# Another order of the same operations in the middle stage of a two-layer hybrid decoder step

## The chip, the cores and the metric

The kernel runs on one core of one Trainium2 chip. The metric is device time in microseconds (us). Before the change it is 1229.5 us, the median of three runs (1227.54 to 1229.52). Engines are named as in the profile: PE is TensorE's matmul, PEld its weight load, DVE is VectorE, ACT is ScalarE, POOL is GpSimd, SP is SyncE, which here issues every DMA; a small q behind a name (SPq) means the sequencer of that engine.

## The reference, cut to what matters

There are two layers. Each layer takes 512 prompt tokens (four tiles of 128 rows) and 64 sample tokens (8 sequences of 8 new tokens, the fifth tile, `S_TILE`) and does this:

```python
h = rmsnorm(x);  z = h @ w_in                      # one product makes all branch columns
q_r, k_r, v_r, g_r, q_lat, c_raw, kpe_raw, g_a = split(z)
# retention: 4 heads, chunks of 128 tokens, one state of 128 x 128 per head
a = (q_r k_r^T) * decay mask;  o = a v_r + q_r S * decay;  S = S * decay + k_r^T v_r
o_r = groupnorm(o) * silu(g_r)                     # sample tokens: 8 states read from state_ret
# latent attention: 4 heads
q = rmsnorm(q_lat) @ w_qb; qn = rmsnorm(q[:, :128]); qp = rope(rmsnorm(q[:, 128:]))
kn = rmsnorm(c @ w_kb); v = c @ w_vb;  kpe = rope(rmsnorm(kpe_raw))
o_a = softmax(mask((qn kn^T + qp kpe^T) * scale)) v * silu(g_a)
# sample tokens attend to 2048 cached rows each, read by page from cache_ckv and cache_kpe
y = concat(o_r, o_a) @ w_out;  x = x + y
```

The outputs are the new x of both kinds of token, the new latent and rotary rows and the new retention states.

## The kernel before, in words

Each engine has its own instruction stream, written out by hand, and the streams meet only at semaphores. A layer has three stages. The first computes z (`tile_products`, L577 to L579 and L587, L588). The middle stage does the retention and the attention of the prompt tokens, the retention of the sample tokens and the preparation of their queries. The last walks over the 8 sample sequences, 8 pairs of pages each (`turn_pair` L1014 and L1018, `pair_keys` L1039), and ends in the output product. The change touches the middle stage only; it stands once in the code and runs in both layers, at about 180 to 292 us and 788 to 899 us of the profiled execution.

The middle stage is a list of calls on each of PE, ACT, DVE and POOL. The order of the list is the order in which that engine does the work: a call whose semaphore has not come holds up all the calls behind it. The parts are these, with t a tile, n one of the 16 (query tile, head) pairs of the prompt attention, and k one of 5 retention steps, of which k=0 is the sample tokens.

- Queries: PE `latents(t)` turns the latents (L668 to L671), ACT `keep_latents` copies them, PE `q_project(t)` (L690), ACT `square_q`, DVE `sum_q`, POOL `qp_root` and `qn_root`, DVE `scale_qp` and `scale_qn`, POOL `rope_q`, PE `q_turn` (L719) and `qp_turn` (L730), ACT `keep_q` and `keep_qp`.
- Keys and values: PE `v_project(t)` (L681), ACT `keep_v`; PE `k_project(t)` (L703), ACT `square_k` (L1375), DVE `sum_k`, POOL `k_root` (L2260), DVE `scale_k` (L1863), PE `k_turn(t)` (L709), ACT `keep_k`.
- Attention: PE `scores(n)` (L849, L850), DVE `attn_max`, ACT `probs`, PE `turn_probs(n)` (L863), ACT `keep_probs` (L1452), PE `attend(n)` (L872), DVE `attn_out`. `scores(n)` waits for `attn_out(n-2)`. `turn_probs` and `q_turn` share PSUM bank 5, so each `turn_probs` waits for the `keep_probs` before it.
- Retention: PE `ret_turn(k)` (L776), ACT `ret_keep` (L1425), PE `ret_scores(k)` (L784), DVE `ret_mask`, PE `ret_out(k)` (L825, L828, L832), DVE `ret_stats` and `ret_state`, POOL `ret_root`, DVE `ret_norm`, POOL `ret_y`. They use banks 6 and 7.
- Sample states: `S0` holds 8 states per head, which SP loads in four DMAs (L459) issued when the last product of the first stage is in PSUM. PE `step_read` (L795) multiplies the sample queries with all of `S0`: it waits for `s0_in` (all four DMAs) and for `ret_mask(0)`, and `ret_out(0)` waits for its copy. `step_update(h)` (L808), DVE `step_add(h)` (L1940), ACT `step_scale(h)` and POOL `step_mask(h)` write the new states. SP stores the new latent rows (L464 to L470) right behind the four loads.
- Hand-over to the last stage: PE `absorb()` (L749) folds the key weights into the sample queries. SP waits for its end (`absorb_ps`, since the page buffers share memory with `S0` and `wkbT`), then loads the 16 pages of sequence 0 in four quarters (L479 reads a page number, L493 and L495 issue), stores the prompt's state (L506), waits for that store to land, loads four parts of `wout` (L513) and only then loads the pages of sequence 1. `first_pages` (L883) and `first_rotary_keys` (L889) turn the first pair of pages inside the middle stage; the former waits for the first quarter, the latter for `ret_norm(S_TILE)`.

The lists of SP and all code of the calls but one small helper stay as they are.

## Time and profile before

| | |
|---|---|
| median of 3 runs | 1229.5 us |
| time of the profiled execution | 1228.56 us |
| its span (first to last instruction) | 1226.7 us |
| PE busy | 1213.5 us, 99% |
| DVE, ACT, POOL busy | 59%, 44%, 35% |
| granted TensorE clock | 1.00 throughout |
| middle stage, both layers alike | about 112 us each |

A busy share of PE counts the modelled end of each matmul, which reaches past the start of the next one. So a short wait is partly covered by it: what PE loses is better read from the distance between the starts of two groups, set against the same group where nothing waits.

### The profile page before, as it was taken

Reading aid. Unit: us, or ns where it says so; the run is one execution under the profiler, and the core shown is the slowest. Engines: PE = TensorE matmul, PEld = TensorE weight load, DVE = VectorE, ACT = ScalarE, POOL = GpSimd, SP = SyncE. Lnnn points to the kernel's source line nnn. Section 1 sums busy time; section 2 is a strip of 40 time slices with the busy share of each in tenths; the row PEclk is TensorE's granted clock in tenths of the full one; section 3 lists DMA queues with packets and bytes.
Section 4 is the critical chain, followed back from the end, with each engine's and each line's share of the span. In section 5 each row is a group of like instructions: output and inputs, shape, how many; then the busy total and the mean of one; then the engine's idle time right before and its main releaser. Section 6 shows DMA issues by size and latency. Waiting matters only on the chain.

```text
span 1226.7 us, 26265 instructions
## 1 busy us (share of the span) xinstructions
PE 1213.5 (99%) x8727; PEld 1122.3 (91%) x8727; DVE 728.6 (59%) x1379; ACT 544.7 (44%) x1443; POOL 435.0 (35%) x632
## 2 busy tenths in 40 slices
PE   8999999999999999999999999999999999999999
PEld 7999995768999999999999999867789999999998
DVE  5556756565666666676454575656556666665752
ACT  6313235444655555562342132453445555555520
POOL 1033055432554545541001220554235554544500
PEclk9999999999999999999999999999999999999999
DMA  6632104003435422210543130320042543222012
GB/s 219 220 94 61 49 24 115 25 2 95 128 89 156 123 82 75 79 44 30 217 134 112 55 110 1 80 83 1 11 143 78 162 123 97 80 74 83 23 58 67
DMA packets 127687, 107.28 MB, mean 87 GB/s; under 512 B 45713, under 2 KB 123682, under 8 KB 127586
## 3 DMA queue, kind: packets, MB, share of 16 engines
q1 hardware_dynamic: 127586, 106.04, 29.3%
q8 instruction: 51, 0.84, 0.3%
q14 instruction: 50, 0.41, 0.1%
HBM read 95.08 MB, written 10.91 MB: 86 GB/s over the span
## 4 chain that ended last, share of the span: by engine, by line
PE 90%; DVE 3%; SPq 2%; ACT 2%; issue 1%; DVEq 1%; POOL 1%; DMA 0%; POOLq 0%; ACTq 0%
PE ps L1039 28%; PE ps L577 10%; PE ps L578 10%; PE ps L579 10%; PE ps L1014 4%; PE ps L690 3%; PE ps L587 3%; PE ps L588 3%; PE ps L1067 2%; PE ps L1048 2%; PE ps L849 1%; PE ps L703 1%; PE ps L850 1%; PE ps L872 1%; PE ps L1018 1%
## 5 line engine op out<-in xcount | busy, mean ns | idle before, releaser
L2094 DVE TENSOR_REDUCE kss<-ksq 128x8 f32<-128x1024 f32 x128 | 156.0, 1219 | 167.6 <-ACT ksq L1572 167.5
L1572 ACT ACTIVATE ksq<-ps 128x544 f32<-128x544 f32 x256 | 160.2, 626 | 192.8 <-PE ps L1039 192.3
L577 PE MATMUL ps<-w_hi,hT_hi 128*128 128x408 f32 (+2 forms) x704 | 241.8, 343 | 2.1 <-DVE w_lo L1685 2.1
L578 PE MATMUL ps<-w_lo,hT_hi 128*128 128x408 f32 (+2 forms) x704 | 239.2, 340 | 0.0
L579 PE MATMUL ps<-w_hi,hT_lo 128*128 128x408 f32 (+2 forms) x704 | 239.0, 339 | 0.0
L1039 PE MATMUL ps<-wq_hi,cT_hi 128*128 128x272 f32 x1024 | 223.2, 300 | 0.0
L2429 POOL TENSOR_TENSOR krs<-kss_t,cst 128x8 f32<-128x8 f32 x128 | 210.3, 1643 | 20.1 <-issue 4.2
L1039 PE MATMUL ps<-wq_lo,cT_hi 128*128 128x272 f32 x1024 | 211.6, 288 | 0.0
L1039 PE MATMUL ps<-wq_hi,cT_lo 128*128 128x272 f32 x1024 | 211.5, 288 | 0.0
L1039 PEld LDWEIGHTS ps<-wq_hi,cT_lo 128*128 128x128 f32 x1024 | 160.3, 189 | 0.0
L1039 PEld LDWEIGHTS ps<-wq_lo,cT_hi 128*128 128x128 f32 x1024 | 160.1, 188 | 0.0
L1039 PEld LDWEIGHTS ps<-wq_hi,cT_hi 128*128 128x128 f32 x1024 | 158.8, 189 | 0.0
L577 PEld LDWEIGHTS ps<-w_hi,hT_hi 128*128 128x128 f32 x704 | 132.1, 188 | 4.1 <-issue 3.0
L578 PEld LDWEIGHTS ps<-w_lo,hT_hi 128*128 128x128 f32 x704 | 132.3, 188 | 0.2
L579 PEld LDWEIGHTS ps<-w_hi,hT_lo 128*128 128x128 f32 x704 | 132.1, 188 | 0.1
L2422 POOL TENSOR_TENSOR kss_t<-kss,cst 128x8 f32<-128x8 f32 x128 | 27.4, 214 | 237.6 <-DVE kss L2094 237.6
L1263 ACT ACTIVATE z<-ps 64x408 f32<-64x408 f32 x16 | 8.1, 509 | 212.1 <-PE ps L588 212.1
L1559 ACT ACTIVATE cT_hi<-ps 128x512 fp32r<-128x512 f32 x126 | 76.6, 608 | 34.6 <-PE ps L1014 34.3
L2086 DVE TENSOR_TENSOR cT_lo<-ps,cT_hi 128x512 fp32r<-128x512 f32 x126 | 86.1, 684 | 0.6
L2254 POOL TENSOR_SCALAR pool_tmp<-stat 128x1 f32<-128x1 f32 (+2 forms) x70 | 14.7, 210 | 190.9 <-ACTq L1238 76.4
L1014 PE MATMUL ps<-cst,ckv 128*128 128x128 f32 x504 | 78.5, 278 | 1.9 <-DVE cT_lo L2086 1.3
L1705 DVE TENSOR_SCALAR z<-ps,x_root 128x408 f32<-128x408 f32 x64 | 39.2, 638 | 67.9 <-PE ps L579 66.6
(217 smaller groups left out, 2013.4 us busy)
## 6 DMA issues: line engine op xcount, KB each, us to landing
ckv<-in_cache_ckv SPq DMA_DIRECT2D x256, 128.0 KB, 2.0
raw<-in_w_in SPq DMA_DIRECT2D x64, 408.0 KB, 4.7
kp<-in_cache_kpe SPq DMA_DIRECT2D x256, 32.0 KB, 1.8
S<-in_state_ret SPq DMA_DIRECT2D x8, 512.0 KB, 6.5
out<-S SPq DMA_DIRECT2D x8, 512.0 KB, 3.3
wout<-in_w_out SPq DMA_DIRECT2D x8, 344.0 KB, 4.0
z<-in_w_out SPq DMA_DIRECT2D x8, 340.0 KB, 4.6
raw<-in_w_out SPq DMA_DIRECT2D x8, 340.0 KB, 4.4
```

Of the source, the lines that this page charges most:

```text
L577: pe.matmul(out, a_hi, b_hi, start=first, stop=False)
L578: pe.matmul(out, a_hi, b_lo, start=False, stop=False)
L579: return pe.matmul(out, a_lo, b_hi, start=False, stop=last)
L587: pe.matmul(out, hT_s[:, c, :], w_h(c), start=c == 0, stop=False)
L1014: m = pe.transpose(ps[:, 0, (2 * j + c) * P:(2 * j + c + 1) * P], ckv[b][:, 2 * q + j, c * P:(c + 1) * P], ident)
L1039: m = pe.matmul(ps[:, 1 + 2 * j + side, 0:CUT], x, w[:, c, w0:w0 + CUT], start=c == 0 and k == 0, stop=c == KC - 1 and k == 2)
L1559: act.activation(cT_hi[:, par, :, :].rearrange("p a n -> p (a n)"), ps[:, 0, :], ACT.Copy)\
L1572: act.activation(ksq[:, q % 2, j, :].rearrange("p (s c) -> p s c", s=2), ps[:, 1 + 2 * j:3 + 2 * j, 0:CUT], ACT.Square).then_inc(kk_sq, 1)
L1705: dve.tensor_scalar(dst, ps[0:n, BANK[t], 0:GW], x_root[:, t:t + 1], None, ALU.mult)\
L2086: dve.tensor_tensor(cT_lo[:, par, :, :].rearrange("p a n -> p (a n)"), ps[:, 0, :], cT_hi[:, par, :, :].rearrange("p a n -> p (a n)").bitc ...
L2094: dve.tensor_reduce(kss[:, hs, 2 * k:2 * k + 2, :], ksq[:, q % 2, :, c0:c0 + HW].rearrange("p j (h k) -> p j h k", h=H), AX.X, ALU.add).th ...
L2429: pool.tensor_tensor(krs[:, hs, c, :], tmp, spread_col(neg_half[:, 0:1]), ALU.pow)\
```

## The change

The lists of the four engines are put in another order. No operation is added or removed, and no semaphore or buffer changes. Two edits are more than a move: DVE's `beside_w(S1, 0)` becomes `first_queries()`, which drains first and stands earlier, and the definitions of two ACT helpers move above the list (one is renamed). Cut to the parts that matter here:

```diff
 # PE
             latents(0)
             turn_wkb()
+            ret_turn(0)
             q_project(0)
-            ret_turn(0)
+            ret_scores(0)
             v_project(0)
-            ret_scores(0)
+            step_read()
             k_project(0)
-            step_read()
-            q_turn(0)
             latents(1)
             ret_out(0)
+            q_turn(0)
             k_turn(0)
             q_project(1)
             qp_turn(0)
             step_update(0)
+            scores(0)
             v_project(1)
-            scores(0)
             scores(1)
             step_update(1)
+            turn_probs(0)
             k_project(1)
-            turn_probs(0)
+            latents(2)
+            attend(0)
+            turn_probs(1)
             step_update(2)
-            turn_probs(1)
-            attend(0)
-            latents(2)
             q_turn(1)
+            scores(2)
             attend(1)
+            k_turn(1)
+            q_project(2)
...
             qp_turn(S_TILE)
-            scores(13)
             turn_probs(12)
+            ret_scores(S_TILE)
             absorb()
-            ret_scores(S_TILE)
+            attend(12)
             turn_probs(13)
-            attend(12)
             ret_out(S_TILE)
+            attend(13)
             scores(14)
-            attend(13)
+            scores(15)
             new_scores()
-            scores(15)
             turn_probs(14)
             first_pages()
+            first_rotary_keys()
+            turn_probs(15)
             attend(14)
-            turn_probs(15)
-            first_rotary_keys()
             attend(15)
 # ACT
             keep_latents(0)
             keep_wkbT()
+            ret_keep(0)
             tanh(0)
+            square_q(0)
             tanh(1)
-            tanh(2)
-            tanh(3)
-            tanh(S_TILE)
-            square_q(0)
-            ret_keep(0)
             keep_v(0)
+            keep_read()
             square_k(0)
-            keep_read()
+            keep_latents(1)
             keep_q(0)
-            keep_latents(1)
...
             probs(14)
+            probs(15)
             keep_probs(14)
-            probs(15)
             first_pages_hi()
             keep_probs(15)
-            first_rotary_keys()
+            keep_first_rotary_keys()
 # DVE
+            def first_queries():
+                dve.drain()
+                beside_w(S1, 0)
+
             clear()
             gates(0)
-            gates(1)
-            gates(2)
-            gates(3)
-            gates(S_TILE)
+            ret_mask(0)
             sum_q(0)
-            ret_mask(0)
...
             ret_mask(S_TILE)
+            gates(3)
             attn_out(12)
             split_absorbed()
+            gates(S_TILE)
+            first_queries()
             ret_stats(S_TILE)
+            attn_out(13)
             ret_state(S_TILE)
-            attn_out(13)
             attn_max(14)
+            attn_max(15)
             ret_norm(S_TILE)
-            attn_max(15)
             new_scores_out()
+            first_pages_lo()
             attn_out(14)
-            beside_w(S1, 0)
-            first_pages_lo()
             attn_out(15)
 # POOL
             pads()
-            step_mask(0)
             qp_root(0)
             qn_root(0)
             rope_q(0)
             k_root(0)
             ret_root(0)
+            step_mask(0)
+            step_mask(1)
...
+            ret_root(S_TILE)
             ret_y(3)
             k_root(S_TILE)
-            ret_root(S_TILE)
             ret_y(S_TILE)
```

In the part of PE's list that is left out, `ret_scores(k)` moves further behind `ret_turn(k)` for k = 1 to 3 (in the list before, `qp_turn` and at most one or two short blocks stand between them; in the new one `scores`, `attend` and projections do), and `scores`, `turn_probs` and `attend` of later n are interleaved in other pairs. On ACT `tanh(2)`, `tanh(3)` and `tanh(S_TILE)` and the four `step_scale` are spread over the stage, and on DVE `gates` likewise.

## Rows read from the trace of the kernel before

**Rows 1.** Busy by stretch, layer 0's middle stage: PE, PEld, DVE, ACT, POOL, clock, DMA.
```profile
180.00:292.00 112.00, 110.20 (x666) 75.83 (x665) 71.16 (x205) 51.95 (x114) 47.30 (x72) 1.00 0.21 56
```

**Rows 2.** Timeline of PE, start of layer 0's middle stage: start, length, instruction, [idle <-releaser].
```profile
179.94 0.38 PE L668 MATMUL ps<-cst,z 128*128 128x128 f32 x2
...
181.82 4.14 PE L690 MATMUL ps<-wqb,qlT 128*128 128x384 f32 x12 [0.19 <-ACT kpeT L1355]
...
189.20 1.98 PE L703 MATMUL ps<-wkb,cT 128*128 128x512 f32 x4
191.12 1.95 PE L795 MATMUL ps<-S,qkT 128*32 128x128 f32 x64
193.00 0.66 PE L719 MATMUL ps<-cst,qn 128*128 128x128 f32 x4
...
196.31 0.66 PE L709 MATMUL ps<-cst,kn 128*128 128x128 f32 x4
```

**Rows 3.** Timeline of SP: the fourth load of S0, in layers 0 and 1.
```profile
182.63 1.59 SPq L459 DMA_DIRECT2D S<-in_state_ret  x1
...
790.24 1.61 SPq L459 DMA_DIRECT2D S<-in_state_ret  x1
```

**Rows 4.** DMA view of the same two issues: size, us from issue to landing.
```profile
S<-in_state_ret SPq DMA_DIRECT2D x1, 512.0 KB, 8.4
...
S<-in_state_ret SPq DMA_DIRECT2D x1, 512.0 KB, 7.4
```

**Rows 5.** Timeline of PE at the same place in layer 1.
```profile
796.88 1.99 PE L703 MATMUL ps<-wkb,cT 128*128 128x512 f32 x4
798.80 1.95 PE L795 MATMUL ps<-S,qkT 128*32 128x128 f32 x64
```

**Rows 6.** Chain that ended last, layer 0's middle stage: start, us on the chain, what.
```profile
225.52 1.72 PE ps L703 x4
...
256.91 0.89 PE ps L784 x8
```

**Rows 7.** Timelines of ACT, POOL and DVE: the steps of the first key tile.
```profile
191.22 0.60 ACT L1375 ACTIVATE ksq_p<-ps 128x512 f32<-128x512 f32 x1 [2.07 <-PE ps L703]
...
192.03 0.68 DVE L1831 TENSOR_REDUCE stat<-ksq_p 128x4 f32<-128x512 f32 x1
...
193.99 1.01 POOL L2260 TENSOR_TENSOR rstat<-pool_tmp,cst 128x4 f32<-128x4 f32 x1
...
195.04 0.69 DVE L1863 TENSOR_TENSOR kn<-ps,rstat 128x512 f32<-128x512 f32 x1 [2.33 <-POOL rstat L2260]
```

**Rows 8.** Timeline of PE: the four largest other waits of layer 0's middle stage.
```profile
208.51 1.13 PE L808 MATMUL ps<-vm,z 32*128 32x512 f32 x4 [0.28 <-DVE S L1940]
...
237.24 1.16 PE L784 MATMUL ps<-qkT 128*128 128x128 f32 x8 [0.23 <-ACT qkT L1425]
...
288.36 1.16 PE L872 MATMUL ps<-V,prT 128*128 128x128 f32 x8 [0.25 <-ACT prT L1452]
...
290.64 1.16 PE L872 MATMUL ps<-V,prT 128*128 128x128 f32 x8 [0.58 <-ACT prT L1452]
```

**Rows 9.** Chain that ended last, layer 0, from absorb to sequence 1's first pages.
```profile
274.44 1.75 PE ps L749 x16
304.35 3.99 DMA out<-S
...
316.38 2.10 DMA ckv<-in_cache_ckv
...
318.53 0.66 PE ps L1014 x4
```

**Rows 10.** The same chain view in layer 1, where it stays on PE.
```profile
882.11 1.73 PE ps L749 x16
```

**Rows 11.** Timelines of SP and PE, layer 1: last first-quarter page of sequence 1, its turn.
```profile
921.40 0.33 SPq L495 DMA_DIRECT2D ckv<-in_cache_ckv  x1
...
925.48 0.61 PE L1014 MATMUL ps<-cst,ckv 128*128 128x128 f32 x4
```

More of the change, by code:

```diff
@@ L936, in _ @@
             turn_probs(4)
-            latents(3)
-            scores(5)
+            ret_scores(1)
             attend(4)
             q_turn(2)
+            scores(5)
+            latents(3)
+            ret_out(1)
+            scores(6)
+            k_turn(2)
             q_project(3)
             turn_probs(5)
-            scores(6)
-            k_turn(2)
+            qp_turn(2)
             ret_turn(2)
             attend(5)
-            qp_turn(2)
-            ret_scores(2)
+            v_project(3)
             scores(7)
             turn_probs(6)
-            v_project(3)
-            ret_out(2)
+            ret_scores(2)
             attend(6)
@@ L955, in _ @@
             turn_probs(7)
-            latents(S_TILE)
             scores(8)
             attend(7)
-            q_project(S_TILE)
+            ret_out(2)
+            latents(S_TILE)
             turn_probs(8)
             scores(9)
-            ret_turn(3)
             attend(8)
             q_turn(3)
+            q_project(S_TILE)
+            turn_probs(9)
+            ret_turn(3)
+            scores(10)
+            attend(9)
+            ret_scores(3)
+            scores(11)
             k_turn(3)
-            ret_scores(3)
-            scores(10)
-            turn_probs(9)
+            turn_probs(10)
             ret_out(3)
-            attend(9)
+            turn_probs(11)
             qp_turn(3)
-            turn_probs(10)
-            scores(11)
             attend(10)
+            q_turn(S_TILE)
+            attend(11)
             k_project(S_TILE)
             scores(12)
-            turn_probs(11)
             ret_turn(S_TILE)
-            attend(11)
-            q_turn(S_TILE)
+            scores(13)
             qp_turn(S_TILE)
-            scores(13)
             turn_probs(12)
+            ret_scores(S_TILE)
             absorb()
-            ret_scores(S_TILE)
+            attend(12)
             turn_probs(13)
-            attend(12)
             ret_out(S_TILE)
+            attend(13)
             scores(14)
-            attend(13)
+            scores(15)
             new_scores()
-            scores(15)
             turn_probs(14)
             first_pages()
+            first_rotary_keys()
+            turn_probs(15)
             attend(14)
-            turn_probs(15)
-            first_rotary_keys()
             attend(15)
@@ L1997, in _ @@
             ret_stats(0)
+            gates(1)
             ret_norm(0)
@@ L2001, in _ @@
             attn_max(0)
+            scale_qp(1)
             attn_max(1)
-            scale_qp(1)
+            scale_qn(1)
             step_add(1)
-            scale_qn(1)
             sum_k(1)
+            attn_out(0)
+            scale_k(1)
+            attn_max(2)
             step_add(2)
-            attn_out(0)
             attn_out(1)
-            scale_k(1)
+            gates(2)
+            attn_max(3)
             step_add(3)
-            attn_max(2)
+            attn_out(2)
             sum_q(2)
-            attn_max(3)
@@ L2015, in _ @@
-            ret_mask(1)
-            attn_out(2)
+            attn_max(4)
             scale_qp(2)
             scale_qn(2)
-            attn_max(4)
+            attn_out(3)
+            ret_mask(1)
+            sum_k(2)
+            attn_out(4)
+            attn_max(5)
+            scale_k(2)
             ret_stats(1)
-            attn_out(3)
             ret_state(1)
-            sum_k(2)
+            attn_max(6)
             ret_norm(1)
-            attn_max(5)
-            attn_out(4)
-            scale_k(2)
+            attn_out(5)
@@ L2028, in _ @@
             sum_q(3)
-            attn_max(6)
-            attn_out(5)
+            attn_max(7)
+            attn_out(6)
+            scale_qp(3)
             ret_mask(2)
-            scale_qp(3)
-            attn_max(7)
+            attn_max(8)
             scale_qn(3)
-            ret_stats(2)
-            attn_out(6)
-            ret_state(2)
-            ret_norm(2)
-            attn_max(8)
             sum_k(3)
             attn_out(7)
+            ret_stats(2)
+            ret_state(2)
+            attn_max(9)
```

131 lines of the change are left out of this document (64 added, 67 removed).

## The prediction

> **What bounds the kernel now.** I read the page's busy shares first, then the busy time by stretch, the chain of waits, the timelines of the middle stage and last the DMA issues. PE is busy in 110.20 of layer 0's 112.00 us, with the clock at 1.00, its upper level [rows 1], so this stage is PE's work plus what PE waits. The middle stage's matmuls are the same before and after. Only waits can be won or lost, in the two layers alike, and whatever sits behind the stage must let a win through.
>
> The waits are larger than the idle brackets say. At the start, `q_project(0)` sits behind the latents' copy [rows 2], the bracket of 0.19, where PE loses 0.35 us by the distance between starts, and each of the next four changes of block costs it another 0.20, the last one at `step_read`. That is 1.15 us up to 191.12. The other waits of size are at `step_update(2)`, before `ret_scores(1)` and (2), and two at the end of the stage [rows 8]. By distance between starts they cost 0.45, 0.30, 0.40, 0.41 and 0.74 us. With the start that is 3.45 us per layer: all that an order without waits could win, 6.9 us in both. Some 3 us more per layer are restarts of about 0.1 us after a semaphore has just come; both orders have them and I leave them.
>
> Two transfers are tied into this stage. The four loads of `S0` are issued when the first stage ends. The fourth starts at 182.63 and takes 8.4 us, so it lands at 191.0 in layer 0; in layer 1 it lands at 790.24 + 7.4 = 797.6 [rows 3, 4]. PE starts `step_read` at 191.12, at the landing, and at 798.80, 1.2 us after it [rows 2, 5]. The other is the page queue. In layer 0 the chain leaves PE at the end of `absorb()` (274.44 + 1.75 = 276.19) and stays on SP and its DMAs until PE takes up sequence 1's first pages at 318.53: 42.3 us that no matmul shortens, and the store of `S` alone is 3.99 of them [rows 9]. PE waited 0.5 us there. So layer 0 is now set by when `absorb()` ends, not by when the middle stage does. In layer 1 `absorb()` ends at 883.84 [rows 10] and the pages land at 921.40 + 2.10 = 923.50, PE wants them at 925.48 [rows 11]: 2.0 us to spare.
>
> **The start, up to `step_read`.** Before, seven blocks of PE precede it; now `k_project(0)` (1.72 us of PE, as its kind in [rows 6]) goes behind it. The other six fill 189.20 - 179.94 = 9.26 us, less their waits of 0.95 (0.35 and three times 0.20) some 8.3. `ret_turn(0)` moved up covers the wait for the latents' copy, so PE reaches `step_read` at about 188.3. `ret_mask(0)`, its other condition, is through at about 187.2, since DVE now does one gate before it, not five. But `S0` is not there before 191.0. The read starts at 191.12 as before, and PE idles 2.8 us in front of it. What was won is lost in this wait, and `k_project(0)`, which used to fill it, has still to be done: **+1.72 us** in layer 0. In layer 1 the read can start 1.1 us earlier than before (797.7 against 798.80): **+0.6 us**.
>
> At this place the Trainium skill says otherwise. Its page "DMA: Bandwidth & Descriptors", section "Anatomy of one DMA", gives 2.0 us plus bytes over 436 GB/s; for four loads of 512 KB that is an estimate of 6.8 us from the first issue, and `step_read` would wait for nothing. The trace disagrees: from the first issue at 180.1 it is 10.9 us in layer 0.
>
> **From the read to `k_turn(0)`.** Its condition is the chain square, sum, root, scale. Their lengths are 0.60, 0.68, 1.01 and 0.69 us [rows 7]; with the root's first step and the hand-overs of 0.1 to 0.2 us I take 3.75 us from the end of `k_project(0)`. In front of `k_turn(0)` PE now has `latents(1)`, `ret_out(0)` and `q_turn(0)`, the blocks that filled 193.00 to 196.31 before [rows 2], 3.1 us without waits. Before, `step_read` lay between as well, so nothing waited. Bounds: 0, if the chain takes as little as its four lengths (2.98), and 1.3, if POOL is late by one more root. I take **+0.65** in both layers.
>
> **The middle.** The waits of 0.45, 0.30 and 0.40 go: `step_update` now stands 3 us or more behind its `step_add`, and `ret_scores` far enough behind `ret_turn` for ACT's copy. Walking down the four lists from `q_project(1)` with the lengths of these operations I find new, smaller ones: `k_turn(1)` 0.5 (DVE does `step_add(1)` ahead of `sum_k(1)`, so its 3.7 us chain faces 3.1 us of PE work), `q_turn(2)` 0.3 and `scores(5)` 0.15 (both roots of tile 2 come late, and `attn_out(3)` now stands behind both scalings), `scores(11)` 0.2, `scores(0)` 0.15. That is 1.3 against 1.15: **+0.15** in both, with bounds -1.15 (none of mine is real) and +2 (as many again that I missed).
>
> **The end.** Between `turn_probs(14)` and `turn_probs(15)` ACT must copy; before, `attend(14)` and `attend(15)` both stood at the copy of their own probabilities. Now `first_pages` and `first_rotary_keys` fill the first gap and `attend(14)` covers the second copy, so 1.15 us shrinks to 0.3, if `ret_norm(S_TILE)` is in time (it stands behind two `attn_max` now, and by my count ends just as PE asks for it): **-0.85**, bounds -1.15 and +0.5.
>
> **The page queue.** `ret_scores(S_TILE)` now goes ahead of `absorb()`: 0.89 us [rows 6]. So `absorb()` ends later by 1.72 + 0.65 + 0.15 + 0.89 = 3.4 us in layer 0 and by 0.6 + 0.65 + 0.15 + 0.89 = 2.3 in layer 1. What PE wins behind `absorb()` it can't use in layer 0: sequence 1 starts when its pages land, 3.4 us later than before. In layer 1 the pages land at 925.8, and PE, whose own path is +0.6 + 0.65 + 0.15 - 0.85 = +0.55, asks for them at 926.0: no wait. The quarters of sequence 0 keep a few tenths of a microsecond or more.
>
> **Sum.** Layer 0 +3.4, layer 1 +0.55, nothing else moves: +3.95 on 1228.56, 1232.5 us. That execution lies 0.94 below the median of 1229.5, and the four times I have (three runs and this one) average 1228.8; on these the sum is 1232.8, which I give.
>
> **The rivals.**
> - *The page queue does not set layer 0.* From `absorb()` to the landing it took 39.7 us in layer 1 and 42.3 in layer 0, for the same transfers. With layer 1's figure the pages of layer 0 land about 2.7 us earlier against the rest, and only PE's own path counts: 1.72 + 0.65 + 0.15 - 0.85 = 1.67, with 0.55 of layer 1 2.2, less the 0.5 us wait that goes: +1.7, 1230.5. For it: the 3.99 us of the store look like chance. Against: it is what this trace shows.
> - *The new waits are not real.* The order has room for everything but `S0`: layer 0's start +1.72, the middle -1.15, the end -1.15. `absorb()` +1.5 in layer 0, which its queue passes on; layer 1 0.6 - 1.15 - 1.15 = -1.7. Sum -0.2: 1228.6. This is the case that ends on the side of "not slower"; it decides at `k_turn(0)` and `k_turn(1)`, which must not wait.
> - *`S0` is there in time.* The loads land before 188.3, as the rule above has it. Then the start is -1.15 per layer. With my other terms layer 0 is at +0.5 (`absorb()`) and layer 1 at -1.2: 1228.1; without the new waits too -1.4 and -3.45: 1223.9. Against it: nothing changes ahead of these loads.
> - *DVE is late at the end.* It has two gates, `first_queries` and two `attn_max` more between `ret_mask(S_TILE)` and `ret_norm(S_TILE)`. If `attn_out(13)` comes after PE asks for `scores(15)`, each microsecond is one of the stage, and with as many missed waits as I found the sum is +8: 1237.
> - *The clock falls after the 2.8 us of idle PE.* The trace shows 1.00 in every stretch, and no such idle time in the stage either. At the lower of the two levels (1.2 against 2.4 GHz) the work would take twice as long; for one k projection and the blocks after it up to `k_turn(0)`, 1.72 + 3.1 us, that is +4.8 in a layer: 1237 to 1242.
>
> The Trainium skill, "TensorE: Matmul & The Clock Gate", section "The HAM clock gate", says that PE's clock halves once PE has been idle for a while; whether 2.8 us is such a while no row of this trace can show.
>
> **How the numbers follow.** Chances: forecast 0.38, queue without effect 0.18, new waits not real 0.16, `S0` in time 0.12, DVE late 0.13, clock 0.03. About 0.2%, 2.5 us, is what a measurement of this kernel can tell from no change: 1227.0 to 1232.0. The forecast lies 0.8 above that bound with an own range of 1231.0 to 1235.0, so some 0.32 of its 0.38 are slower; with DVE late, the clock and a little of the second case that makes 0.52. Faster needs `S0` in time or the middle without waits and luck in layer 0's queue: 0.15. The rest, 0.33, is no change. Range 1227.0 to 1237.0.
>
> **What would show each step.** An idle bracket of 2 to 3 us before the first `step_read` in layer 0 and 1.5 to 2 in layer 1, released by the DMA of `S`. Waits of half a microsecond before `k_turn(0)` and `k_turn(1)`. None at `step_update(2)` nor before `ret_scores(1)` and (2). `absorb()` ending 99 to 100 us after the stage's first matmul in layer 0, against 96.2 now, and the first turn of sequence 1 about 42 us behind it, with an idle bracket of over 1 us. If `step_read` starts without a wait, the forecast is wrong at its first step; if the middle stage ends earlier than its 111.7 us of before and the total is still longer, the page queue is all of it.

## The result, and the profile after

| | before | after |
|---|---|---|
| median of 12 runs | 1227.83 us (1227.27 to 1229.52) | 1229.85 us (1227.83 to 1233.41) |
| time of the profiled execution | 1228.56 us | 1229.79 us |
| span | 1226.7 us | 1227.9 us |

The ratio is 1.0018, with an interval of 1.0010 to 1.0025: slower, by 2.0 us where 3.95 were forecast. The direction held, the size was twice too large. The twelve times of the new kernel also lie over 5.6 us, those of the old one over 2.3.

The page of the kernel after; PE's busy time is 0.5 us longer than before and its clock stays at its upper level.

```profile
span 1227.9 us, 26267 instructions
PE 1214.0 (99%) x8727; PEld 1122.9 (91%) x8727; DVE 728.2 (59%) x1379; ACT 544.2 (44%) x1443; POOL 435.4 (35%) x632
PEclk9999999999999999999999999999999999999999
```

Busy time by stretch, both layers' middle stages, with the columns of [rows 1]:

```profile
180.00:292.00 112.00, 110.48 (x668) 76.23 (x667) 71.38 (x206) 51.69 (x114) 48.11 (x72) 1.00 0.20 55
788.00:900.00 112.00, 110.48 (x665) 76.24 (x665) 71.14 (x205) 51.69 (x114) 47.74 (x72) 1.00 0.21 55
```

PE is busier in the stretch than in [rows 1] (110.20). So it waits less there, and the loss must lie outside this stretch. The timeline of PE at the start of layer 0's middle stage answers to [rows 2]:

```profile
180.63 0.38 PE L668 MATMUL ps<-cst,z 128*128 128x128 f32 x2
...
187.58 1.98 PE L681 MATMUL ps<-wvb,cT 128*128 128x512 f32 x4
190.32 1.96 PE L795 MATMUL ps<-S,qkT 128*32 128x128 f32 x64 [0.76 <-DMA S<-in_state_ret]
192.20 1.98 PE L703 MATMUL ps<-wkb,cT 128*128 128x512 f32 x4
...
197.76 0.66 PE L709 MATMUL ps<-cst,kn 128*128 128x128 f32 x4 [0.33 <-DVE kn L1863]
```

Count from the stage's first matmul. The read starts at 190.32 - 180.63 = 9.69 us, against 11.18 before, behind a wait for `S0`; `k_turn(0)` starts at 17.13, against 196.31 - 179.94 = 16.37. In the rest of the layer's stage one idle bracket is left, at `k_turn(1)`:

```profile
213.32 0.66 PE L709 MATMUL ps<-cst,kn 128*128 128x128 f32 x4 [0.27 <-DVE kn L1863]
...
290.02 2.01 PE L872 MATMUL ps<-V,prT 128*128 128x128 f32 x16
291.87 0.38 PE L1014 MATMUL ps<-cst,ckv 128*128 128x128 f32 x2
```

The four waits of [rows 8] are gone: both `attend` calls at the end stand as one group of 16 matmuls without a bracket. The last matmul of `absorb()` starts 97.31 us into the stage (95.96 before). The stage ends, with the first turn of the last stage at L1014, at 291.87 - 180.63 = 111.24 (111.70 before). PE got through this stage 0.46 us sooner and the kernel became slower.

The chain that ended last shows where, in the same places as [rows 9], and under it the timeline of PE at sequence 1's first turn:

```profile
276.49 1.75 PE ps L749 x16
...
307.11 2.50 DMA out<-S
317.67 2.37 DMA ckv<-in_cache_ckv
```

```profile
320.09 0.66 PE L1014 MATMUL ps<-cst,ckv 128*128 128x128 f32 x4 [1.89 <-DMA ckv<-in_cache_ckv]
```

`absorb()` ends at 278.24 and sequence 1 starts 41.9 us later, at 139.45 us of the stage (138.59 before), after PE has idled for 1.89. In layer 1 the chain stays on PE as in [rows 10], and the turn starts at 137.39 without a bracket, 0.47 sooner than before ([rows 11]: 925.48 - 787.62 = 137.86):

```profile
926.51 0.61 PE L1014 MATMUL ps<-cst,ckv 128*128 128x128 f32 x4
```

From the middle stage's first matmul to the end of the page walk layer 0 takes 375.55 us (374.75 before) and layer 1 373.38 (373.86). With 0.69 us more ahead of layer 0's stage (180.63 against 179.94; PE's first product of that layer comes at 10.15 us instead of 9.46), and 0.22 outside all this, that is the 1.23 us between the two executions.

### The profile page after: what moved, and what is told of

It reads as the page before. It is cut to its first block, busy times and chain, and to the rows that moved or that the text cites. A ratio compares the mean times of both kernels' runs of the same rounds, so it can differ in the third digit from the quotient of the medians.

```text
span 1227.9 us, 26267 instructions
## 1 busy us (share of the span) xinstructions
PE 1214.0 (99%) x8727; PEld 1122.9 (91%) x8727; DVE 728.2 (59%) x1379; ACT 544.2 (44%) x1443; POOL 435.4 (35%) x632
## 4 chain that ended last, share of the span: by engine, by line
PE 77%; issue 9%; DVE 4%; POOL 3%; SPq 2%; POOLq 2%; DVEq 1%; ACT 1%; DMA 0%; ACTq 0%
PE ps L1039 28%; PE ps L577 7%; PE ps L578 7%; PE ps L579 7%; PE ps L1014 4%; PE ps L690 3%; PE ps L1067 2%; POOL rstat L2264 2%; PE ps L587 2%; PE ps L588 2%; PE ps L1048 2%; PE ps L872 1%; PE ps L849 1%; PE ps L850 1%; PE ps L1018 1%
## 5 line engine op out<-in xcount | busy, mean ns | idle before, releaser
L1014 PE MATMUL ps<-cst,ckv 128*128 128x128 f32 x504 | 78.5, 278 | 3.2 <-DMA ckv<-in_cache_ckv 1.9
```

The source lines that it names most:

```text
L1014: m = pe.transpose(ps[:, 0, (2 * j + c) * P:(2 * j + c + 1) * P], ckv[b][:, 2 * q + j, c * P:(c + 1) * P], ident)
```

## The experiments

Each line is a kernel; the kernel before had medians of 1227.83 to 1229.16 beside them, so the ratios are to be compared, not the times; those with a ratio were timed in rounds beside the kernel before, the others run once beside it. "Queue" is one edit on SP, "front" and "end" are parts of the order; all are shown below.

| kernel | us | ratio to before (95%) |
|---|---|---|
| after, the result above | 1229.85 | 1.0018 (1.0010 to 1.0025) |
| before + queue | 1228.44 | 0.9998 (0.9989 to 1.0007) |
| after + queue | 1227.70 | 0.9997 (0.9988 to 1.0006) |
| after, k projection ahead of the read | 1229.63 | 1.0006 (0.9997 to 1.0015) |
| before + the end of after | 1227.23 | 0.9987 (0.9978 to 0.9996) |
| before + end + queue | 1226.62 | 0.9987 (0.9979 to 0.9996) |
| after with the front of before | 1226.90 | 0.9991 (0.9983 to 1.0000) |
| the same + queue + `absorb()` first | 1225.77 | 0.9982 (0.9973 to 0.9991) |
| after with the front of before + queue | 1224.88 | 0.9973 (0.9963 to 0.9982) |
| after, stores behind `S0` | 1229.81 | one run |
| after, `S0` behind the stores | 1245.66 | one run |
| before, `S0` behind the stores | 1233.40 | one run |
| after, `absorb()` first | 1230.27 | one run |
| after again | 1232.16 | one run |
| before again | 1229.07 | one run |

**The page queue, taken out.** The theory: layer 0 is set by the landing of sequence 1's pages, which counts from `absorb()`. The edit lets the first quarter of these pages go ahead of the wait for the state's store and of the `wout` loads; it runs in both kernels.

```diff
             sp.wait_ge(y_ret, TILES)
+            load_seq(1, 1, None, (0,))
             sp.wait_ge(state_out, 16 * (L + 1))
             for k in range(4):
                 sp.dma_start(wout0[:, k, :, :], ...).then_inc(wout0_in, 16)
-            load_seq(1, 1, None)
+            load_seq(1, 1, None, (1, 2, 3))
```

> The kernel before, with SP's page queue shortened: the first quarter of sequence 1's pages is issued ahead of the four wout loads and of the wait for the state's store, instead of behind both. Nothing else is changed. Theory (page queue: in layer 0 sequence 1 starts when SP's queue behind absorb() has brought its pages, 42 us later): PE's wait of 0.5 us before the first turn of sequence 1 in layer 0 goes, the pages land some 6 us before they are wanted, the median falls by about 0.5 us to 1227.3, and the spread of the times shrinks. Rival (the queue is no bound, its wait a chance of one execution): the median stays at 1227.8 with the same spread. Second rival: wout now comes too late for the split in the first sequence, and PE or ACT waits there: up to 2 us slower.

> The changed kernel with the same edit of SP's queue. In its trace the middle stage ends 0.45 us earlier than before in both layers, and layer 0 is yet 0.8 us longer, with an idle PE before sequence 1. Page queue theory: that wait goes, layer 0 gains what layer 1 gains, the median falls from 1229.85 to about 1227 (0.9 us under the kernel before) and the spread (1227.8 to 1233.4) shrinks to that of before. Rival (the new order loses its time elsewhere, in the first or last stage): it stays near 1229.8 with its spread.

The timelines of PE at sequence 1's first turn in layer 0, first before + queue, then after + queue (this edit adds a line, so L1014 is L1015):

```profile
318.00 0.61 PE L1015 MATMUL ps<-cst,ckv 128*128 128x128 f32 x4
```

```profile
317.07 0.61 PE L1015 MATMUL ps<-cst,ckv 128*128 128x128 f32 x4
```

Neither has a bracket: 137.89 and 137.40 us into the stage, which is PE's own pace (seven turns of 3.74 us behind the first). In the new kernel the edit is worth 1.0018 - 0.9997, about 2.6 us, and the intervals don't meet. In the old one it shows nothing, for there the queue was at most 0.7 us late in layer 0 and in some executions not at all (below). So the queue is real, and it cost the new order about as much as its whole measured loss (the two ratios come from different sets of runs, each beside the kernel before).

**The read.** The k projection goes back ahead of the read and its square ahead of the read's copy.

```diff
 # PE
             v_project(0)
-            step_read()
             k_project(0)
+            step_read()
 # ACT
-            keep_read()
             square_k(0)
+            keep_read()
```

> The changed kernel with k_project(0) back ahead of step_read() on PE and square_k(0) ahead of keep_read() on ACT; all else as changed. Theory (S0's landing and the chain of the first keys cost the new order its start): PE reaches step_read at about 10.1 us of the stage, just behind the landing at 9.65, and does not wait; k_turn(0) no longer waits; it starts at about 15.3 instead of 17.13. absorb() is 1.8 us earlier in both layers, layer 0's queue with it: 1229.85 - 3.6 = 1226.2. Rival (the idle time only lets the helpers catch up, and the waits move to k_turn(1) and the attention): half of that, about 1228.

The timeline of PE, layer 0:

```profile
190.89 1.98 PE L703 MATMUL ps<-wkb,cT 128*128 128x512 f32 x4 [0.69 <-ACT V L1360]
192.81 1.95 PE L795 MATMUL ps<-S,qkT 128*32 128x128 f32 x64
...
196.00 1.05 PE L822 MATMUL ps<-read,cst 128*32 128x512 f32 x4 [0.43 <-ACT read L1430]
...
198.49 0.60 PE L709 MATMUL ps<-cst,kn 128*128 128x128 f32 x4
```

The wait for `S0` is gone, and two for ACT's copies stand in its place, 0.69 and 0.43 us. So the start at 15.3 us that the theory expected didn't come, nor did its 1226.2 us. `k_turn(0)` starts at 17.21 us in both layers, whether `S0` lands at 10.93 or at 10.05. That is 0.08 later than the profiled execution of after, where `S0` landed at 9.65, and 1.26 sooner than the late one below. The interval reaches from no change to 1.5 thousandths and meets that of after, so by time alone it decides nothing. What the trace shows is a fixed 17.21 us where the new start has 17.13 to 18.47, and still 0.84 more than before: these two calls alone don't bring the old start back.

**The end alone.** The kernel before, with the order of after from `ret_out(S_TILE)` on, on PE, ACT and DVE. PE's part:

```diff
             ret_out(S_TILE)
-            scores(14)
             attend(13)
-            new_scores()
+            scores(14)
             scores(15)
+            new_scores()
             turn_probs(14)
             first_pages()
-            attend(14)
+            first_rotary_keys()
             turn_probs(15)
-            first_rotary_keys()
+            attend(14)
             attend(15)
```

> The kernel before with the changed kernel's end of the middle stage alone (PE from ret_out(S_TILE), ACT from probs(14), DVE from split_absorbed; the gates and the rest stay). The middle stage should end 0.9 us earlier in both layers. Page queue theory: absorb() does not move, so layer 0 gives nothing and layer 1 all of it: 1227.8 - 0.9 = 1226.9. Rival (no queue: both layers give): 1226.0. Rival (DVE late at the end): ret_norm(S_TILE) or attn_out(13) makes a wait and the stage ends no earlier: 1227.8.

> The kernel before with the changed kernel's end of the middle stage and with SP's shortened page queue. The end alone made both stages 0.92 us shorter, but layer 0 kept 0.4 of it only, since it waited 1.0 us for the pages of sequence 1. Page queue theory: with the queue shortened the wait goes, layer 0 keeps all of its 0.92 and the former 0.5 too; the sum of both layers is 0.9 + 1.4 = 2.3 us under the kernel before (1226.9 where that has 1229.2). Rival (the two edits don't add up, since the pages come late elsewhere): 1.2 us under it as with the end alone.

The timeline of PE at the end of this stage in before + end:

```profile
287.95 0.32 PE L889 MATMUL ps<-cst,kp 128*128 128x128 f32 x1
288.46 0.63 PE L863 MATMUL ps<-cst,pr 128*128 128x128 f32 x4 [0.18 <-ACT prT L1452]
288.92 2.01 PE L872 MATMUL ps<-V,prT 128*128 128x128 f32 x16
290.77 0.60 PE L1014 MATMUL ps<-cst,ckv 128*128 128x128 f32 x4
```

The stage ends at 110.78 us instead of 111.70 in either layer, 0.92 less. DVE is not late: no bracket of 0.15 us or more stands before any block of this end but the 0.18 for ACT's copy. Layer 1's walk ends 0.94 earlier, layer 0's only 0.58: there sequence 1 starts at 138.05, when its pages land, and PE would have asked at 136.96. With the queue edit the landing no longer counts and the turn starts at 136.94. By time that further step is too small to see.

**The front.** After, with the order of before up to `k_turn(0)`, on ACT and DVE too; only `ret_turn(0)` stays ahead of `q_project(0)`. PE's part:

```diff
             ret_turn(0)
             q_project(0)
-            ret_scores(0)
             v_project(0)
-            step_read()
+            ret_scores(0)
             k_project(0)
+            step_read()
+            q_turn(0)
             latents(1)
             ret_out(0)
-            q_turn(0)
             k_turn(0)
```

> The changed kernel with the former order from v_project(0) to k_turn(0) on PE, ACT and DVE (ret_turn(0) stays ahead of q_project(0)), so that every step but the first stands as before. My last trial put k_project(0) straight behind v_project(0), where it waits for the copy of the bank they share; here ret_scores(0) stands between. Theory (the start is where the new order loses; what it wins later stays): step_read starts at about 10.1 us, or at the landing of S0 where that is later, k_turn(0) 5.2 us behind it at 15.3 to 16.2 instead of 17.13, absorb() ends 1 to 1.8 us earlier in both layers, and the median falls by 2 to 3 us against the changed kernel, to 1226.5 on the scale where the kernel before has 1229.2. Rival (the wait only moves on, to k_turn(1) or the attention): absorb() stays at 97.4 us of the stage.

> All that the experiments point to: the changed kernel with the former start (as in the trial beside this one), absorb() ahead of ret_scores(S_TILE) again, and SP's shortened page queue. Per layer: start 0.2 to 1.1 us under the kernel before, middle 0.3, end 0.92; layer 0 another 0.5 for the wait that goes. Sum 3.3 to 5 us under the kernel before: 1224.2 to 1225.9 where that has 1229.2. Rival (start and end share their gain with other waits): no more than the 2.3 us of the end with the queue.

> The changed kernel with the former start and SP's shortened page queue, and with ret_scores(S_TILE) ahead of absorb() as the change has it. In the trial with absorb() first, absorb() ended only 0.34 us earlier and the middle stage 0.54 us later, so that move did not pay. Theory (the parts add up): middle stage 110.5 us in layer 0 and 110.0 in layer 1, no wait at sequence 1, each layer 1.2 to 1.6 us under the kernel before and layer 0 another 0.5 where its page queue was late: 0.5 to 0.9 us under that trial, 2.8 to 3.5 us under the kernel before, 1224.7 where that has 1227.9. Rival (at this size the first stage's scatter is all that is left): no difference from that trial's 1225.8.

The timeline of PE in layer 0 of after with this front:

```profile
189.45 1.98 PE L703 MATMUL ps<-wkb,cT 128*128 128x512 f32 x4
191.80 1.95 PE L795 MATMUL ps<-S,qkT 128*32 128x128 f32 x64 [0.36 <-DMA S<-in_state_ret]
...
196.99 0.66 PE L709 MATMUL ps<-cst,kn 128*128 128x128 f32 x4
```

`S0` landed at 11.11 us here, and the wait behind the k projection is 0.36 instead of 2. `k_turn(0)` starts at 16.35, and at 15.91 in layer 1, where `S0` was there in time. Against 1.0018 for after the ratio is 0.9991, 0.0027 less or 3.3 us, and the intervals don't meet: the start is where the change loses. The middle and the end of the new order are worth keeping, though by this ratio alone only just (its interval ends at 1.0000).

With the queue edit too the kernel is at 0.9973, the lowest ratio of all; its interval meets neither that of the front alone nor that of before + queue. Its PE asks for sequence 1 at 136.52 and 136.18 us of the stage and never waits there (timeline of PE, layers 0 and 1):

```profile
318.11 0.61 PE L1015 MATMUL ps<-cst,ckv 128*128 128x128 f32 x4
...
923.28 0.61 PE L1015 MATMUL ps<-cst,ckv 128*128 128x128 f32 x4
```

**`absorb()` first.** After, with `absorb()` again ahead of `ret_scores(S_TILE)`.

```diff
             turn_probs(12)
-            ret_scores(S_TILE)
             absorb()
+            ret_scores(S_TILE)
             attend(12)
```

> The changed kernel with absorb() ahead of ret_scores(S_TILE) again, as it stood before; nothing else. One look. Page queue theory: absorb() ends 0.9 us earlier, at 96.4 us of the stage in place of 97.3; the middle stage ends where it did (111.2); the pages of sequence 1 in layer 0 land 0.9 us earlier by the queue (some 41.8 to 42.4 us behind absorb(), so at 138.3 to 138.9 of the stage), and PE's wait there shrinks by as much. Layer 1 is unchanged. Rival (the queue follows the end of the middle stage): no change of the turn of sequence 1.

The timeline of PE in this kernel, layer 0, at the two moved calls and at the end of the stage:

```profile
276.54 1.97 PE L749 MATMUL ps<-qnT,wkbT 128*128 128x64 f32 x16 [0.31 <-issue]
278.34 1.11 PE L784 MATMUL ps<-qkT 128*128 128x128 f32 x8
...
290.74 0.63 PE L863 MATMUL ps<-cst,pr 128*128 128x128 f32 x4 [0.18 <-ACT prT L1452]
```

Of the 0.89 us that `ret_scores` takes, `absorb()` won only 0.34: from `k_turn(0)` to its last matmul it is 79.84 us instead of 80.18, since it now starts behind an idle time of its own, 0.31 us, for which the profile shows no releaser. And the stage ends 0.55 later, 94.66 us behind `k_turn(0)` against 94.11. So the new place of `ret_scores(S_TILE)` is the better one where PE's own pace decides. The two kernels with the old front and the queue edit point that way, 0.9982 with `absorb()` first and 0.9973 without, though their intervals overlap. Where the page queue decides it stays open: here sequence 1 starts at 139.29 and 138.56 us of the stage, in after again below at 140.44 and 138.06. That is 0.65 less in sum with `absorb()` first, because the queue of layer 0 was 2.1 us shorter (39.62 us from the last matmul's start to the landing, against 41.74).

**The landing of `S0`.** First the stores behind it on SP are held until it has landed, then the order is turned round.

```diff
             sp.wait_ge(lat_ok, TILES)
+            sp.wait_ge(s0_in, 16 * H)
             sp.dma_start(ckv_p ...
```

> The changed kernel with one wait more on SP: the four stores of latent and rotary rows are held until all four loads of S0 have landed. One look. In twelve loads traced so far (two layers of six kernels) the last landed 9.4 to 10.9 us after the first was issued, with the stores' packets among theirs. Theory (the loads share the 16 DMA engines with the stores): the last load lands at 7.5 to 8.5 us, and step_read starts without a DMA wait at about 8.4 us of the stage instead of 9.69. Rival (the loads are bound by their own packets or by memory): it lands at 9.4 or later as before, and step_read waits as before.

> The changed kernel with the four loads of S0 issued behind the four stores of latent and rotary rows, so that S0 lands later: by some 2.5 us, about 12 us after the start of the stage. One look; it prices the wait at step_read. Theory (each microsecond that S0 is late is one of PE's, and absorb() passes it on): step_read starts with the landing, at about 12.1 us instead of 9.69, and k_turn(0), absorb() and in layer 0 the first turn of sequence 1 each move by the same 2.4 us. Rival (the helpers catch up while PE waits, so that waits further down go): absorb() moves by half of it or less.

> The kernel before with the four loads of S0 issued behind the four stores, as tried on the changed kernel, where S0 then landed at 13.4 us of the stage, PE idled 4.5 us before step_read and the granted clock was 0.5 for the following 3.4 us. Here k_project(0) stands ahead of step_read, so PE should idle about 2.4 us there. Theory (the former start is the less sensitive one): step_read at 13.4, k_turn(0) at 18.6 (22.5 in the changed kernel), absorb()'s last matmul at 98.2. If the clock stays at 1.00, idle time of this length does not cost it; if it falls, both orders pay and the read itself takes 3.5 us for 1.9.

With the stores held back `S0` lands 9.57 and 9.61 us into the stage, as in the profiled execution of after (9.65, 9.64). With the four stores ahead of it, it lands 9.65 to 10.51 us behind its own first issue (four layers of two kernels), no longer than the 9.4 to 10.9 seen elsewhere. So no trace shows that the stores matter to the loads. That they don't is not shown either: with the stores held back the loads take 9.37 and 9.42 us from the first issue, the least of all traces, if by under 0.1 us, and it is one execution.

The two last kernels answer another question, what a longer wait does. First after, then before with `S0` behind the stores, the timeline of PE and under it the clock (the last three numbers of a window are clock, DMA share and GB/s):

```profile
195.18 3.53 PE L795 MATMUL ps<-S,qkT 128*32 128x128 f32 x64 [4.54 <-DMA S<-in_state_ret]
...
204.21 0.66 PE L709 MATMUL ps<-cst,kn 128*128 128x128 f32 x4 [0.34 <-DVE kn L1863]
```

```profile
194.00:198.00 4.00, 2.82 (x56) 2.60 (x60) 0.00 (x0) 0.00 (x0) 1.07 (x3) 0.63 0.02 5
```

```profile
193.60 3.62 PE L795 MATMUL ps<-S,qkT 128*32 128x128 f32 x64 [2.22 <-DMA S<-in_state_ret]
```

```profile
194.00:198.00 4.00, 4.00 (x70) 3.62 (x61) 0.69 (x1) 0.73 (x1) 1.01 (x2) 0.61 0.00 0
```

Behind these waits the granted clock fell to its lower level (1.2 GHz, half of 2.4) and `step_read` took 3.53 and 3.62 us instead of 1.96. In the new order's layer 0 the landing came 2.4 us later than in after again below (13.42 against 10.99), and `k_turn(0)` 4.0 us later: the other 1.6 is this fall.

The new order's 1245.66 us are 13.5 more than after again. Layer 1 gives 6.8 of them: 2.8 for the later landing (12.96 against 10.16), 2.9 for a fall behind a wait of 4.08, 1.1 for a longer page queue. Layer 0 gives 6.2, and there the clock fell a second time, behind a wait of only 2.05 us at sequence 1. The first pair of turns then takes 5.31 us instead of 3.78:

```profile
326.69 0.66 PE L1014 MATMUL ps<-cst,ckv 128*128 128x128 f32 x4 [2.05 <-DMA ckv<-in_cache_ckv]
...
332.00 0.61 PE L1014 MATMUL ps<-cst,ckv 128*128 128x128 f32 x4
```

```profile
327.00:332.00 5.00, 5.00 (x32) 5.00 (x29) 0.69 (x1) 1.48 (x4) 1.64 (x2) 0.66 0.32 83
```

**Both kernels again.** For what a second execution of each looks like.

> The kernel before, unchanged: a second trace of it, to see what differs between two executions. Theory (the times of one kernel scatter by 1.7 us because of the first stage of layer 0 and the page queue, not the middle stage): both middle stages last 111.7 us again within 0.05 us, with step_read at 11.2 us and absorb() ending at 96.2; what differs lies before the start of layer 0's middle stage or at the turn of sequence 1. Rival: step_read moves with the landing of S0 by up to 1 us.

> The changed kernel, unchanged: a second trace of it. In the first one S0 landed at 9.65 us of the stage in both layers, while nine of the twelve other loads of layer 0 traced so far landed at 10.9 to 11.1. Theory (the median execution of the changed kernel is one with a late S0, and the first trace a lucky one): step_read in layer 0 starts at about 11.0 us, k_turn(0) 7.44 us behind it at 18.4, absorb()'s last matmul at 98.6, the middle stage ends at 112.5, and the first turn of sequence 1 comes at 138.7 or, with a slow page queue, up to 141. Rival (the first trace is typical, and the median's 2 us come from elsewhere): step_read at 9.7 us again.

After again, PE in layer 0 at the start and at sequence 1, and the clock behind the wait:

```profile
181.48 0.38 PE L668 MATMUL ps<-cst,z 128*128 128x128 f32 x2
...
192.51 1.96 PE L795 MATMUL ps<-S,qkT 128*32 128x128 f32 x64 [2.10 <-DMA S<-in_state_ret]
...
199.95 0.66 PE L709 MATMUL ps<-cst,kn 128*128 128x128 f32 x4 [0.33 <-DVE kn L1863]
...
321.92 0.66 PE L1014 MATMUL ps<-cst,ckv 128*128 128x128 f32 x4 [1.54 <-DMA ckv<-in_cache_ckv]
```

```profile
192.00:197.00 5.00, 4.49 (x76) 3.12 (x78) 1.00 (x4) 1.61 (x2) 2.86 (x5) 1.00 0.09 23
```

Here `S0` landed at 10.99 us, the wait is 2.10 and `k_turn(0)` starts at 18.47, 2.10 later than before. The old order, run again, has the read at 11.18, `k_turn(0)` at 16.37 and the end at 111.70, to the hundredth as in its first trace, with `S0` at 10.95 instead of 11.07 and at 10.18 instead of 9.98 in layer 1. (Both executions also started layer 0's stage late, at 181.48 and 181.31 us, for a cause ahead of the change that the last section shows.) That is the difference between the two: the old order absorbs what these loads do (in layer 0 by no more than 0.07 to 0.3 us: the landings lie at 10.87 to 11.11, its read at 11.18), the new one hands it on.

## Why the prediction was partly wrong, step by step

The waits that the forecast named at `step_read`, at `k_turn(0)` and at sequence 1 of layer 0 are there. What failed is the size of two terms of its sum: the middle, taken as +0.15 us per layer and measured as -0.30, and the time from `absorb()` to the landing of sequence 1's pages in layer 0, carried over as 42.58 us and measured as 42.10 in the profiled execution and 41.74 in the second one.

The steps, as places in the stage, with the change against the trace of before; "two" is the second execution of after.

| step | predicted | after, layers 0 / 1 | two, layers 0 / 1 |
|---|---|---|---|
| `k_turn(0)` (start and its chain) | +2.37 / +1.25 | +0.76 / +0.76 | +2.10 / +1.27 |
| middle | +0.15 | -0.30 / -0.30 | -0.30 / -0.30 |
| `ret_scores` ahead of `absorb()` | +0.89 | +0.89 | +0.89 |
| `absorb()` | +3.4 / +2.3 | +1.35 / +1.36 | +2.69 / +1.87 |
| end | -0.85 | -0.92 / -0.92 | -0.93 / -0.91 |
| first turn of sequence 1 | +3.4 / +0.55 | +0.86 / -0.47 | +1.85 / +0.20 |

(The middle is the distance from `k_turn(0)` to the last matmul of `absorb()`, 80.18 us in all four layers against 79.59, less the 0.89 of [rows 6]; the end is what is left up to the first turn, with that 0.89 given back.)

**What held.** `step_read` waits for `S0`, the k projection is then still to be done, and nothing else costs as much. From the read to `k_turn(0)` it is 7.44 us in all four layers of the new order, so with the landing that I read, 11.0 us, the step comes out at +2.10 against 2.37. The wait at `k_turn(0)` is real (0.33 by the bracket, 0.42 by distances: 7.44 less the 5.19 of before and the 1.83 of the k projection), where I took 0.65. The end gave 0.92 for 0.85 forecast. The queue hands `absorb()`'s delay on in layer 0. (PE reached `step_read` at about 8.9 us of the stage and not at 8.4, so it idled 2.10 where I had 2.8: the blocks in front of it won 0.33 us by the new order and not 0.95. With `S0` later than either it does not touch the sum, but `S0` in time would have brought less than I wrote.)

**What failed, and by how much.** Take the second execution, where `S0` landed as late as in the forecast: the turn of sequence 1 moved by 1.85 + 0.20 = 2.05 us, where 3.95 were forecast. The 1.90 between them are these terms.
- *The middle*, 0.45 per layer, 0.9 in all. I listed five new waits worth 1.3 us, and two came about as large as I had them. `k_turn(1)` starts 0.66 us behind an `attend` group that elsewhere takes 0.22: 0.44 where I took 0.5. `scores(0)` starts 1.21 us behind `step_update(0)`, and the block behind `step_update(1)` 1.06: 0.15, as forecast. Timeline of PE, after:

```profile
202.66 1.13 PE L808 MATMUL ps<-vm,z 32*128 32x512 f32 x4
203.87 0.46 PE L849 MATMUL ps<-knT,qnT 128*128 128x128 f32 x2
...
206.64 1.13 PE L808 MATMUL ps<-vm,z 32*128 32x512 f32 x4
207.70 0.33 PE L863 MATMUL ps<-cst,pr 128*128 128x128 f32 x1
...
212.66 0.39 PE L872 MATMUL ps<-V,prT 128*128 128x128 f32 x2
```

  The other three, 0.65 together, did not come: no other start of the middle is late by more than 0.12 us, which is little above the restarts of both orders. There I walked down the lists with each engine's operations in series and let the late ones add up; the engines had more slack than that. What is left up to -0.30, some 0.9 for the old waits that went, is less than the 1.15 I took. So the rival "not real" (-1.15) lies farther from -0.30 than the forecast, and was wrong about `k_turn(0)` too. The middle and `ret_scores` together were 1.04 in the forecast and 0.59 in the traces; the experiment with `absorb()` first splits these 0.59 in another way, +0.25 for the middle (79.84 against 79.59) and 0.34 for the move, since without it `absorb()` would have waited. By that split it was the 0.89 that was too large.
- *The start*, 0.27 in layer 0.
- *The queue's length.* The sum carried over the time from `absorb()` to the landing of sequence 1's pages from the one trace I had, 42.58 us from the last matmul's start in layer 0. In the other traces with the usual queue it is 39.6 to 42.3, in either layer, for the same transfers; in this one 41.74. That is 0.84 us of layer 0, and it is the part of the first rival that came true. The store of `S`, 3.99 us in [rows 9], was 2.50 in after. In before again the turn started at 137.88 in layer 0, without a wait: the old kernel lost 0.7 us in the trace from which I summed that it did not lose in the next one. The store is not all of it: after has a store of 2.50 and yet 42.10. SP's timeline shows the rest, in its issues of single pages. Nearly all take 0.33 to 0.4 us, but some take far more, first in before, then in after:

```profile
289.40 1.83 SPq L495 DMA_DIRECT2D ckv<-in_cache_ckv  x1
```

```profile
305.19 1.88 SPq L495 DMA_DIRECT2D ckv<-in_cache_ckv  x1
```

  Up to sequence 1's pages the issues of over 0.6 us cost layer 0 1.5 us above the usual 0.33 in before, nothing in before again, 2.2 in after and 1.9 in after again. In the eight traces with `ret_scores(S_TILE)` ahead of `absorb()` it is 1.5 to 2.2, in the eight with `absorb()` first 0 to 1.5. So the length of the queue in layer 0 may go with the order and not only with chance. What holds SP up there stays open.
- *Layer 1* is then within 0.35 of its forecast, by the same middle term against 0.13 us of waiting for pages that I had not seen.

These are 0.90, 0.27, 0.84 and some -0.11 of small change (the end, and the layer 1 wait). The profiled execution of after is another 1.66 us better at these two turns: `S0` landed 1.34 us sooner in layer 0 and 0.52 in layer 1, and its queue in layer 0 was 0.36 longer.

**Where the time of a typical run goes.** With `S0` loaded at its usual place the landing in layer 0 is 10.87 to 11.11 us in eleven traces and 9.57 to 9.65 in three (after, after + queue, stores held back); in layer 1 it is 9.6 to 10.2 in all. With the common landing the new order loses 2.05 us by the places above, counted from the first trace of before, and 2.76 counted from the second, whose queue was shorter; the medians differ by 2.02. So that the first figure meets the medians is in part luck, and that the late landing is what a typical run has is argued from few traces, for the other runs have none. The front experiment and the queue experiment, which were timed, say the same without it: each alone removes the loss.

**The other rivals.** "`S0` in time" fell: `step_read` waited in both traces of after, 0.76 and 2.10 us in layer 0. The estimate from the Trainium skill ("DMA: Bandwidth & Descriptors", section "Anatomy of one DMA") was 6.8 us from the first issue; the 14 traces with the loads at their usual place have 9.4 to 10.9. That section fits its rule to single DMAs issued by GpSimd, and these are four in a row from SP: I carried it over to a case that it does not speak of, and these figures do not speak against it. "DVE late" fell with the end experiment. "The clock falls" did not happen in either trace of after (1.00 behind a wait of 2.10 us) and did in the two kernels with `S0` behind the stores, behind waits of 2.22, 4.54, 4.08 and once 2.05 us: nearer than its 3% said. The Trainium skill, "TensorE: Matmul & The Clock Gate", section "The HAM clock gate", has the clock halve behind an idle engine, and those two traces agree.

## What to carry to other kernels

A forecast from one trace must not carry over a transfer's time as a constant when the change removes what hid it: put its spread in the sum, from both layers and from a second execution of the same kernel. When work is moved from in front of a wait for a DMA to behind it, as the k projection of 1.83 us was here, all of it can be lost when the DMA lands late, and the schedule also starts to scatter as the DMA does: look at the range of the runs, not only at the median. In a list with engines in series, count a wait only where the chain is longer than all that stands beside it; of five small ones found by hand two came. And a call that is moved ahead of another costs it only what the other would not have waited anyway: 0.34 us here for a call of 0.89.

## What the runs showed of the hardware

- The same four 512 KB loads landed 9.4 to 9.5 us (three traces) or 10.7 to 10.9 us (eleven) behind the first issue in layer 0, and never in between, in the 14 traces with the loads at their usual place. With the stores sent ahead it was 10.51 twice, with the stores held back 9.37 once. What chooses stays open.
- An issue of one page load held SP for 0.33 us as a rule and for 0.7 to 1.9 now and then, and such issues made up as much as 2.2 of the 39.6 to 42.6 us from `absorb()` to the landing of sequence 1's pages in layer 0.
- The granted clock fell in the first stage in 6 of 16 traces, old and new orders alike, and the middle stage of layer 0 then starts at 181.28 to 181.72 us instead of 179.66 to 180.65. The two windows, before and before again:

```profile
10.00:16.00 6.00, 5.73 (x37) 5.30 (x36) 4.53 (x8) 4.80 (x10) 1.64 (x4) 1.00 1.04 298
```

```profile
10.00:16.00 6.00, 5.73 (x26) 5.25 (x25) 4.33 (x8) 4.55 (x9) 0.77 (x2) 0.72 1.04 298
```

  PE had idled 1.87 us in front of its first product in the one and 2.12 in the other; over all traces the clock held behind 1.62 to 2.11 us and fell behind 1.80 to 2.33, so the length of the wait alone does not decide it. Later in layer 0 it held behind a wait of 2.10 and fell behind one of 2.05.
- This fall explains the two groups in the times of one kernel. For 76 later runs of the kernel before the record has the mean granted clock. 45 have 1.000, with a median of 1227.8 us, and 31 have 0.999 or 0.998, with 1229.4; 43 of the former lie under 1229.0 and 29 of the latter above. It also explains why the medians of the kernel before in the experiments differ: 17 of 33, 9 of 29 and 5 of 13 runs had the lower figure. It does not explain the loss. Three of the twelve runs of the new kernel had it (1231.37, 1233.04 and 1233.41 us). The other nine have a median of 1229.7, the nine lower times of the old kernel 1227.7.
